# Memory keys and values computed inside the score loop of a two-block transformer kernel

## The reference

```python
u = rms_norm(h, norm_mix)
qa, ka, va, qb, kvb, gb, gate_a, gate_b = split(u @ w_in)
o_a = diff_attention(qa, ka, va, ...)          # 8 score maps of 256x256
o_b = nsa_attention(qb, kvb, sigmoid(gb), ...) # 16 score maps
merged = sigmoid(gate_a) * (o_a @ w_branch_a) + sigmoid(gate_b) * (o_b @ w_branch_b)
h = h + merged @ w_out
# cross attention to a memory of 256 rows, 4 heads of 128
q  = rms_norm(h, norm_cross) @ wq
kv = rms_norm(mem, norm_mem) @ wkv             # 256x1024: keys and values
h = h + softmax(q k^T / sqrt(128)) v @ wo
h = h + peer_ffn(rms_norm(h, norm_ffn), ...)   # top 16 of 16384 experts, 8 heads
out = rms_norm(h, norm_final)
```

## Time and profile before

| what | value |
|---|---|
| median of 3 runs | 1564.78 us (1564.63 to 1565.46) |
| profiled execution | 1564.94 us |
| its span | 1562.8 us |
| PE busy in the span | 1268.1 us |
| DVE, ACT, POOL busy | 742.9, 468.2, 273.3 us |
| mean granted TensorE clock | 0.913 of full |

### The profile page before, as it was taken

The page is one execution under the profiler, slowest core; times in us unless marked ns, Lnnn a source line. Parts: engine busy times, 40 slices in busy tenths (PEclk is TensorE's granted clock), DMA queues, the critical chain, the costliest instruction groups (busy, mean ns, idle before and its releaser), DMA issues.

```text
span 1562.8 us, 21200 instructions
## 1 busy us (share of the span) xinstructions
PE 1268.1 (81%) x8509; PEld 744.5 (48%) x8509; DVE 742.9 (48%) x1768; ACT 468.2 (30%) x1248; POOL 273.3 (17%) x287
## 2 busy tenths in 40 slices
PE   7999999999999887988999887678755645655556
PEld 7787656665555447976666544245411111111112
DVE  5544212221121116357641666575767676767454
ACT  5832111110010016455542134242323232323222
POOL 1000000000000001000000133334443333333341
PEclk9999999999999998989999989989977687687778
DMA  9448999999999995542162399999999999999996
GB/s 368 161 182 355 427 423 427 426 422 428 424 425 425 424 401 225 201 177 108 66 258 93 149 397 422 421 390 399 421 421 421 420 421 421 421 421 421 422 421 270
DMA packets 64438, 544.09 MB, mean 348 GB/s; under 512 B 6608, under 2 KB 7120, under 8 KB 12368
## 3 DMA queue, kind: packets, MB, share of 16 engines
q1 hardware_dynamic: 26016, 273.84, 42.6%
q0 software_dynamic: 38016, 268.45, 41.7%
q10 hardware_dynamic: 304, 0.39, 0.1%
HBM read 541.61 MB, written 1.05 MB: 347 GB/s over the span
## 4 chain that ended last, share of the span: by engine, by line
PE 42%; DMA 40%; DVE 8%; ACT 5%; issue 4%; POOL 1%; DVEq 0%; POOLq 0%; SPq 0%; ACTq 0%
PE PS L197 41%; DMA AR<-in_uv,CO 25%; DMA AR<-in_w_up 12%; DVE AR L2267 2%; DMA Wk<-in_w_up 2%; PE PS L207 2%; ACT HI L186 1%; DVE Wk L1593 0%; POOL AR L2476 0%; DMA XN<-in_uv,CO 0%; ACT Wk L2169 0%; ACT SM L2163 0%; DVE Wk L1596 0%; DVE LO L193 0%; DMA CO<-in_const 0%
## 5 line engine op out<-in xcount | busy, mean ns | idle before, releaser
L197 PE MATMUL PS<-AR,Wk 64*64 64x512 f32 (+4 forms) x2288 | 430.0, 726 | 198.5 <-ACT Wk L2169 185.9
L2267 DVE CUSTOM_DVE_ANT_0 AR<-AR,PS 128x1024 f32<-128x1024 f32 x210 | 255.6, 1220 | 186.5 <-DMA AR<-in_uv,CO 168.5
L197 PEld LDWEIGHTS PS<-AR,Wk 64*64 64x64 f32 (+3 forms) x2288 | 120.1, 159 | 456.3 <-ACT Wk L2169 293.4
L2476 POOL DMA_INDIRECT AR<-in_uv,CO x202 | 193.6, 958 | 318.4 <-PE PS L197 279.6
L197 PE MATMUL PS<-AR 128*64 128x256 f32 (+3 forms) x1944 | 220.3, 383 | 16.9 <-DMA AR<-in_w_up 13.9
L197 PEld LDWEIGHTS PS<-AR 128*64 128x64 f32 (+2 forms) x1944 | 137.0, 139 | 105.5 <-DMA AR<-in_w_up 20.3
L308 POOL TENSOR_TENSOR ST<-ST 128x2 f32<-128x2 f32 (+3 forms) x14 | 11.3, 807 | 802.5 <-DVE ST L1114 477.5
L2159 ACT ACTIVATE RW<-SM 128x2 f32<-128x2 f32 (+1 forms) x132 | 27.0, 205 | 394.3 <-DVE SM L2267 375.5
L197 PE MATMUL PS<-Wk,AR 128*128 128x128 f32 (+2 forms) x976 | 114.7, 308 | 4.3 <-DMA Wk<-in_w_up 2.2
L197 PEld LDWEIGHTS PS<-Wk,AR 128*128 128x128 f32 (+1 forms) x976 | 98.8, 176 | 34.7 <-issue 17.3
L992 DVE TENSOR_TENSOR AR<-AR,PS 128x256 f32<-128x256 f32 x32 | 13.5, 422 | 199.5 <-ACT AR L849 199.5
(11 more groups left out here) (295 smaller groups left out, 1651.3 us busy)
## 6 DMA issues: line engine op xcount, KB each, us to landing
AR<-in_w_gate SPq DMA_DIRECT2D x28, 2048.0 KB, 14.8
AR<-in_w_up SPq DMA_DIRECT2D x27, 2048.0 KB, 14.7
AR<-in_w_down SPq DMA_DIRECT2D x27, 2048.0 KB, 14.7
AR<-in_w_in SPq DMA_DIRECT2D x14, 2048.0 KB, 10.1
Wk<-in_w_up SPq DMA_DIRECT2D x5, 2048.0 KB, 14.7
Wk<-in_w_down SPq DMA_DIRECT2D x5, 2048.0 KB, 14.7
Wk<-in_w_gate SPq DMA_DIRECT2D x4, 2048.0 KB, 14.7
AR<-in_w_pq SPq DMA_DIRECT2D x4, 2048.0 KB, 8.5
```

The lines of the kernel that those rows point to most:

```text
L197: return pe.matmul(o, l, r, start=start, stop=stop, skip_group_check=True)
L2267: t = dve.tensor_tensor_reduce(r, r, P(6 if g < 128 else 2, 2), 1.0, 0.0, ALU.mult, ALU.add, DT[:, g:g + 1])
L2476: pool.indirect_dma_start(RING[k], None, uv, bass.IndirectOffsetOnAxis(ap=IDX[:, g:g + 1], axis=0)).then_inc(g_in[k], 16)
```

## The change

Part one: the memory's work moves from behind the loop into it. Its square sums, means and scaling (ACT, DVE, POOL) go from the end of the loop to steps 12 to 14, its turning to steps 16 and 17, with eight copies into one plain fp32 tile `MX2` shared by ACT and DVE. Keys are made in steps 18 to 21, values in steps 22 to 25, by plain fp32 matmuls on the units as they landed: 32 of 256 columns and 16 of 512 columns. The high and low parts of kv0, kv1 and of the memory are gone.

Part two: gates start at step 0 in place of the `spare` matmuls. Steps 0 to 5 carry 9, 9 and 6 matmuls as before; in steps 6 to 17 an output takes two steps of 12. The first two quarters of b6 are split ahead of the loop: on ACT they stand before the two copies of `VB`, for which PE waits at the head of the loop.

Part three: behind the loop the branch products are reordered, and the first sigmoids move to step 23. The loads are reordered: kv1 takes slot 3, o20 comes after it in that slot, and kv1, cq, co, o20 and pq0 are issued within the loop.

```diff
-                ("wb", rows4(w_b), 1, None), ("kv0", w_ckv[0], 2, 0), ("o20", w_out2[0], 3, None), ("o21", w_out2[1], 7, None),
-                ("kv1", w_ckv[1], 8, 1), ("cq", w_cq[0], 2, None), ("co", rows4(w_co), 4, None), ("pq0", w_pq[0], 5, None),
+                ("wb", rows4(w_b), 1, None), ("kv0", w_ckv[0], 2, 0), ("kv1", w_ckv[1], 3, 1), ("o21", w_out2[1], 7, None),
+                ("cq", w_cq[0], 2, None), ("co", rows4(w_co), 4, None), ("o20", w_out2[0], 3, None), ("pq0", w_pq[0], 5, None),
...
+        def unit_part(n):
+
+            if n < 6:
+                return "g", n // 3, ((0, 3), (3, 6), (6, 8))[n % 3]
+            if n < 18:
+                return "g", n // 2 - 1, ((0, 4), (4, 8))[n % 2]
+            if n < 22:
+                return "k", n - 18, (0, 8)
+            if n < 26:
+                return "v", n // 2 - 11, ((0, 4), (4, 8))[n % 2]
+            return None, None, (0, 0)
...
+                elif kind == "k":
...
+                    w = raw("kv0").rearrange("p (c n) -> p c n", c=8)
+                    t = matvec(pe, P(4 + k % 2)[:, 0:256], lambda c: w[:, c, 128 * k:128 * k + 128], lambda c: MX2[:, c, :], 8)
+                elif kind == "v":
...
+                    for c in range(c0, c1):
+                        t = mm(pe, P(4 + k), MX2[:, c, xs], w[:, c, :], c == 0, c == 7)
...
             evac(kV, "kv", (2, 3, 2, 3))
+            high_quarters(act, "b6", b_act, range(2))
             for tt in range(2):
                 act.wait_ge(*b_pe.at(f"vb{tt}"))
...
-            for name, step in (("cq", "k3"), ("co", "k3"), ("pq0", "v1"), ("pq1", "b11")):
...
```

More of the change, by code:

```diff
@@ L1360, in mixers2_pe @@
                         mm(pe, P(i % 2)[:, 128:384], lq[r, m, 128:256], rk[r, mk, 0:256], True, True).then_inc(*b_pe.up(f"score{i}"))
-                if n < FIRST_GATE:
-                    spare(pe, 3, 10)
-                else:
-                    k, (c0, c1) = gate_part(n)
-                    j, tt = k // 2, k % 2
-                    wh, wl = halves_of(f"b{6 + j}")
-                    xs = slice(tt * 128, tt * 128 + 128)
-                    if c0 == 0 and k:
-                        pe.wait_ge(*b_act.at(f"g{(k - 1) // 2}{(k - 1) % 2}"))
-                    for c in range(c0, c1):
-                        if tt == 0 and c % 2 == 0:
-                            pe.wait_ge(*b_dve.at(f"b{6 + j}.{c // 2}"))
-                        t = three(pe, P(3), X2[0][:, c, xs], X2[1][:, c, xs], wh[:, c, :], wl[:, c, :], c == 0, c == 7)
-                    if c1 == 8:
-                        t.then_inc(*b_pe.up(f"g{j}{tt}"))
+                unit_pe(n)
                 m = weighted(n - 2)
@@ L1456, in mixers2_act @@
             for n in range(27):
-                if n > FIRST_GATE and (n - FIRST_GATE) % 3 == 0:
-                    gate_out(gate_part(n)[0] - 1)
+                name, kind, k = unit_done(n - 1)
+                if kind == "g":
+                    gate_out(k)
+                elif kind:
+                    act.wait_ge(*b_pe.at(name))
+                    act.activation(*((ckT[:, k, :], P(4 + k % 2)[:, 0:256]) if kind == "k" else (CV[:, k, :], P(4 + k))), ACT.Copy).then_inc(
+                        *b_act.up(name))
                 for i in (n, n + 1) if n < 24 and n % 2 == 0 else ():
@@ L1481, in mixers2_act @@
                     t.then_inc(*b_act.up(f"osq{tt}"))
-                if n in gate_highs:
-                    name, quarters = gate_highs[n]
-                    if name in ("b8", "b9"):
-                        act.wait_ge(*b_pe.at("g01" if name == "b8" else "g11"))
-                    high_quarters(act, name, b_act, quarters)
-                if n == 22:
+                elif n == 12:
                     act.wait_ge(ld_mem, 16)
                     square_sum(act, MM[:, 0, :], junk[:, 0, :], ST[:, 24:25]).then_inc(*b_act.up("sqm"))
-            gate_out(7)
+                elif n == 14:
+                    act.wait_ge(*rms.at("mem"))
+                    act.activation(MM[:, 1, :], MM[:, 1, :], ACT.Copy, scale=ST[:, 25:26]).then_inc(*b_act.up("mem1"))
+                elif n in (16, 17):
+                    act.wait_ge(*b_pe.at(f"tm{n - 16}"))
+                    for c in range(4 * n - 64, 4 * n - 62):
+                        act.activation(MX2[:, c, :], memory_chunk(c), ACT.Copy, scale=sm["g_mem"][:, c:c + 1]).then_inc(*b_act.up(f"y{c}"))
+                elif n == 23:
+                    act.wait_ge(*b_act.at("g31"))
+                    sigmoids(act, 0)
+                if n in HIGHS:
+                    name, quarters = HIGHS[n]
+                    if name in HIGHS_BEHIND:
+                        act.wait_ge(*b_pe.at(HIGHS_BEHIND[name]))
+                    high_quarters(act, name, b_act, quarters)
             act.wait_ge(*b_pe.at("val23"))
@@ L1857, in halves_pe @@
             cross_out_pe(pe, 0, 3).then_inc(*l_pe.up("w00"))
-            cross_out_pe(pe, 1, 0).then_inc(*l_pe.up("w10"))
-            branch_pe(pe, "a", 1, 1, 4).then_inc(*l_pe.up("a11"))
-            branch_pe(pe, "b", 1, 1, 5).then_inc(*l_pe.up("b11"))
+            cross_out_pe(pe, 1, 4).then_inc(*l_pe.up("w10"))
             pe.wait_ge(*l_dve.at("w10"))
-            turn_half_pe(pe, H[:, 0, :], (1, 2), l_pe.up("tp0"))
+            turn_half_pe(pe, H[:, 0, :], (5, 2), l_pe.up("tp0"))
             pe.wait_ge(*l_act.at("p0"))
@@ L1949, in branch @@
                 dve.tensor_tensor(SGA[:, tt, cs], SGA[:, tt, cs], SGB[:, tt, cs], ALU.add).then_inc(*l_dve.up(f"sx{tt}{j}"))
[L1951 to L1953 removed]
+            for j in range(2):
+                branch(0, j, (4 + j, 6 + j))
             dve.wait_ge(*l_pe.at("tx0"))
             chunks_evac_dve(dve, 0, (2, 3), None, range(4, 8)).then_inc(*l_dve.up("x0"))
[L1956 removed]
             dve.wait_ge(*b_pool.at("h1"))
```

246 lines of the change are left out of this document (127 added, 119 removed).

## The result

| | kernel before | changed kernel |
|---|---|---|
| median | 1565.46 us (1564.63 to 1569.72, 7 runs) | 1570.26 us (1567.97 to 1572.9, 7 runs) |
| profiled execution, its span | 1564.94, 1562.8 us | 1568.0, 1565.9 us |
| mean granted TensorE clock | 0.913 | 0.911 |

The ratio is 1.0035, 95% interval 1.0021 to 1.0049. The changed kernel is slower by a third of a per cent. That lies inside the predicted range (1560.5 to 1571.5), but outside its likeliest case, "within 0.2%"; it fell to the side that had 0.33. Two executions of the kernel before, timed beside e5 to e8, took 1893.6 and 1897.3 us at a granted clock of 0.63; they are left out of every ratio here.

A forecast was written before the change was run, and what follows sets the result against it. DMA bounds the kernel's last stage, so the first fetch sets the end, and PE is the chain up to it. Head +3.0, loop +19.5 and behind it -21.3 sum to +1.2 us on 1564.94: 1566.0 us, range 1560.5 to 1571.5.

The forecast's parts named there:

- likeliest case: Whole kernel: time within 0.2% of the kernel before either way, 1561.7 to 1567.9 us, chance 0.45.
- the side that had 0.33: Whole kernel slower than 1567.9 us: clock at the head, weight or late loads, or loop and bare chain at upper bounds.
- The frame: Last stage, full of transfers, keeps its 677 us, so whatever moves the first fetch moves the end one for one.
- the end of the loop: Sign: first branch product at 799 to 805 us, not 781; wrong if before 798 or after 806.
- the stretch behind it: Sign: from the first branch product to tp0's eight transposes 67 us, not 88; wrong if not 65 to 69.
- Head: Steps 0 to 5: loop starts 3.9 us later, step 6 is reached 3.0 us late, bounds 0.5 and 6.
- rival (b): Head of the loop: idle holes lower PE's clock, also in steps 6 to 13; +6 us, 1572, chance 0.18.
- Rest of the loop: From step 6 on: memory's keys, values and turning make the loop 19.5 us longer, bounds 17 and 22.
- Rival (a): Loop: longer units shrink the 7.1 us of bank 3 waits; 5.5 us less, 1560.5, chance 0.22 with companions.
- Behind the loop: Up to tp0: 25.1 us of work gone, 3.8 given back in four bare hand-overs, net 21.3 us gained.
- (c): Steps 18 to 25: slowed by weight loads of 128 columns; 3 us, 1569, chance 0.05 together with (d).
- (d): Loop: a load lands late for step 18 or 22 and stops it; 5 us, 1571, chance 0.05 with (c).

The follow-up runs named there:

- e5: Changed kernel with both reorderings, gate copy ahead of ACT's next quarter and branch products cut into pieces behind the loop: 1563.81 us, ratio 0.9996.
- e8: Changed kernel unaltered, timed again in more rounds: 1570.39 us, ratio 1.0046; its profiled execution took 1579.73 us.
- e9: Changed kernel with only 20 spare matmuls added in each of its two holes at the head of the loop: 1570.2 us, ratio 1.0028.
- e3: Changed kernel with three branch products cut into pieces and laid into the bare hand-overs behind the loop: 1566.94 us, ratio 1.0018.
- e12: Kernel before, unaltered, timed against itself: 1565.6 us against 1563.97 us, ratio 1.0004.
- e1: Changed kernel with ACT copying a gate out of bank 3 before it makes the next unit's high quarter: 1566.24 us, ratio 1.0013.
- e6: e5 with 20 spare matmuls in each of the two holes at the head of the loop: 1560.32 us, ratio 0.9974.
- e11: e7 with 14, 10 and 20 spare matmuls ahead of three waits at the head of the loop: 1560.52 us, ratio 0.9968.
- e7: e5 with ACT copying VB before it rounds the two quarters of b6: 1563.22 us, ratio 0.9999.
- e10: Kernel before without its six groups of ten spare matmuls in steps 0 to 2: 1566.56 us, ratio 1.0013.

## Why the prediction was right and where it was off

**The frame held.** The last stage kept its length, the first fetch decides the end, and the change moved 20 us out of the stretch behind the loop and 20 into the loop. The prediction had the net at +1.2 us; the stages give +4.4 from T0 to the first fetch, less 0.75 that came ahead of T0 and 0.6 in the last stage, both within what equal kernels show. Of the signs put down, the end of the loop (803.1), the stretch behind it (68.3) and the fetch stage (675.9 against 677) came as said; missed were the first scores (668.4, not 669.5 to 670), one pair of 10.9 us where 10.5 was the most, and the first fetch, 3.7 us after 886.3 and not within 3. The step that failed is the head.

**Head: +3.0 forecast, +4.3 measured.** The late start was right (3.9 forecast, 3.6 measured). Wrong was the price of the clock. The sum charged 0.3 us for the first hole, and nothing for the second, behind which it let step 3's matmuls cost no more than before. By e9, which has spare matmuls in both, the first cost 11.57 - 10.85 = 0.7 and the second 8.55 - 5.88 = 2.7 us; one execution of each, so these two are estimates. That the clock may fall after idle was written down, and the rival (b) named both holes; both fell, as the fence of the head shows. The Gelu's result let PE go on 5.8 us later than before, counted from T0, and the scores of step 4 came 7.0 later where I had 4 to 5. Steps 4 and 5 gave 2.7 of it back (8.3 us for 11.0; I had 9.6), which was luck: in e8 the same two steps took 11.9. So rival (b) was right in kind and worth, in this execution, 1.3 us more than the forecast; e8 is an execution in which it took its full price, 4.5 us on top at the head and 1.6 in steps 12 and 13, where (b) had put a further fall. This is what the Trainium skill ("TensorE: Matmul & The Clock Gate", part 1) would have me expect of idle PE time, that the throttled level is the default. The trace agrees at both holes of the head (first scores 1.65 us instead of 0.93; split matmuls 0.43 us apart behind the second), though in e3 the first scores still took 0.93 behind 4.27 us of idle, and the matmuls after them started 0.43 apart.

**Rest of the loop: +19.5 forecast, +19.9 measured.** The waits for bank 3 came out at 7.3 us against 7.1. A step of values, four plain chunks, took 3.54 us where a step of gates, four chunks of three split matmuls, took 2.85: a factor of 1.24, as the 1.25 in the sum. The Trainium skill's 4 passes for true fp32 ("FP8 and Floating Point Precision", TensorE Precision Notes) would give 1.33, 3.8 us for such a step (an estimate); the measured row lies below it. The price of 0.43 us for 256 columns doesn't follow from the quotient given for it, which is 0.385; measured in a step of keys it is 3.56 / 8 = 0.445. The 19.5 was chosen between two sums, 20.6 and 18.6, and that it was met so closely is in part luck: no low stretch fell in this loop, where I had charged half of one, and e8, with the same waits, took 101.06 - 79.47 = 21.6. The kernel before had one low stretch in its profiled execution, and, by e12, has two in others. Rival (a) fell as put, since longer units didn't shorten the waits; e1 shows that the order on ACT does.

**Behind the loop: -21.3 forecast, -20.0 measured.** The four hand-overs idle 0.78 + 1.26 + 0.69 + 0.79 = 3.5 us, against 3.8 in the sum, and the two of before stand unchanged at 1.2 and 0.7. So 1.6 us are missing elsewhere. One half is a price of a bare hand-over beyond its idle: the last row ahead of it isn't overlapped by the next. The transposes of tz0 last 1.16 us and all of it counts here, where in e3 the next row starts 837.06 - 836.06 = 1.00 behind them; the cross queries count 7.38 here and 845.92 - 838.78 = 7.14 there. That is 0.16 to 0.24 each, 0.8 for the four (an estimate). The other half comes of cutting the pieces out by the starts of their neighbours. Ahead of the keys 16 branch products took 13.34 us; here 20 took 820.38 - 803.11 = 17.27, so 16 take 13.8, 0.5 more, with no split product behind them. The scores took 1.54 us up to the start of v1 and take 851.70 - 849.87 = 1.83 here, 0.3 more. e3 shows the same thing from the other side: covering 4.0 us of idle brought 4.35.

**The rivals (c) and (d)** fell: steps of keys and values run at the priced pitch, and PE waits for no load in the loop.

**From the stages to the median.** The stages say +3.1 us, the medians +4.8 (and e8's ratio +7). The profiled executions are single draws: one of the changed kernel at 1568.0, one at 1579.7, with equal waits and different clocks. The median of 1570.26 us stays inside the predicted range by 1.2 us, because rival (b) had set its upper end; the sum itself had 1566.0. What I can't settle is how much of the median's extra is owed to the missing spare matmuls. Four pairs point the same way: e6 below e5 by 3.5 us, e11 below e7 by 0.31% (timed on different chips, so only the ratios compare), e10 above the kernel before by 0.13%, e9's ratio below the changed kernel's two. The first two are nearly clear and clear by their intervals; the last two, which bear on this question, are not.

## What to carry to other kernels

Work moved into a nearly full stretch of the same engine costs there what it saved elsewhere; what it can gain are the holes, and a hole is filled by the order on the engine that ends it (here, ACT's copy before its next quarter: 4.3 us), not by longer work around it. When work leaves a chain, look for what it had covered, and cut the remaining independent work into pieces of about the hand-overs' length (4.35 us here). Where PE's clock falls after idle, read two or more executions before pricing a head: one trace said +3.1 us, another of the same kernel +14.8.
